# Four weight chunks of an expert kernel loaded in ten transfers each

## The reference

```
logits = xt @ w_router + b_router
top_val, top_idx = lax.top_k(logits, 4)            # 4 of 32 experts for each token
gates = softmax(top_val)
# for each expert e and its tokens xb:
h = xb @ w_gate_up[e] + b_gate_up[e]               # 1024 -> 2048
gate, up = minimum(h[:, :1024], 7), clip(h[:, 1024:], -7, 7)
out = ((up + 1) * gate * sigmoid(1.702 * gate)) @ w_down[e] + b_down[e]
y[token] += gates * out
```

## Time and profile before

| | us |
|---|---|
| median of 3 runs | 1215.03 (1214.45 to 1215.11) |
| the profiled execution | 1215.55 |
| its span, first to last instruction | 1213.8 |
| PE busy in the span | 1157.7 |
| PE waiting for DMA, 550 to 1190 us | 34.9 |

### The profile page before, as it was taken

One profiled execution on the slowest core, in us unless ns is written; L12 is line 12 of the kernel. 1 busy time (PEld: TensorE's weight loads), 2 busy tenths in 40 slices (PEclk: granted clock), 3 DMA queues, 4 the chain that ended last, 5 costly groups with the idle time before them and its releaser, 6 DMA issues.

```text
span 1213.8 us, 14228 instructions
## 1 busy us (share of the span) xinstructions
PE 1157.7 (95%) x5861; PEld 613.1 (51%) x5861; DVE 301.0 (25%) x700; ACT 143.0 (12%) x284; POOL 45.2 (4%) x80
## 2 busy tenths in 40 slices
PE   9999999999999999999998998989998989899996
PEld 7888678886434445353434343434343434354332
DVE  4343311223122222222222122211221212122212
ACT  2122111002010100001010101010101010001112
POOL 3032410000000000000000000000000000000000
PEclk9999999999999999999999999999999999999999
DMA  9753775484999999999999999999999999999995
GB/s 319 244 208 95 243 258 221 139 345 174 414 427 426 421 426 431 426 431 430 429 430 425 431 427 435 425 435 422 434 425 433 427 432 427 435 424 430 426 420 224
DMA packets 59884, 451.31 MB, mean 372 GB/s; under 512 B 3778, under 2 KB 34798, under 8 KB 40353
## 3 DMA queue, kind: packets, MB, share of 16 engines
q1 hardware_dynamic: 56576, 439.60, 87.4%
q0 software_dynamic: 2896, 10.11, 2.4%
q10 hardware_dynamic: 344, 0.61, 0.1%
HBM read 444.46 MB, written 6.08 MB: 371 GB/s over the span
## 4 chain that ended last, share of the span: by engine, by line
PE 73%; DMA 22%; SPq 2%; issue 1%; DVE 1%; ACT 0%; POOL 0%; DVEq 0%; POOLq 0%
PE psum L1040 30%; DMA ring<-in_w_gate_up 20%; PE psum L976 19%; PE psum L1051 7%; PE psum L1115 7%; PE psum L1143 2%; SPq L561 2%; DMA ring<-in_w_down 2%; PE psum L1105 1%; PE psum L1144 1%; PE psum L1041 1%; PE psum L842 0%; PE psum L857 0%; PE psum L1141 0%; PE psum L830 0%
## 5 line engine op out<-in xcount | busy, mean ns | idle before, releaser
L1040 PE MATMUL psum<-ring,x_T 128*64 128x512 f32 x992 | 458.4, 611 | 26.3 <-DMA ring<-in_w_gate_up 19.4
L1041 PE MATMUL psum<-ring,x_T 128*64 128x512 f32 x992 | 458.6, 611 | 0.0
L1040 PEld LDWEIGHTS psum<-ring,x_T 128*64 128x64 f32 x992 | 131.6, 140 | 285.2 <-issue 273.1
L1051 PE MATMUL psum<-ring,act_T 128*64 128x512 f32 x960 | 212.6, 595 | 14.5 <-DMA ring<-in_w_down 14.5
L976 PE MATMUL psum<-ring 128*128 128x264 f32 (+1 forms) x768 | 182.0, 392 | 0.6 <-issue 0.6
L976 PEld LDWEIGHTS psum<-ring 128*128 128x128 f32 x768 | 143.3, 190 | 30.3 <-issue 4.2
L1051 PEld LDWEIGHTS psum<-ring,act_T 128*64 128x64 f32 x960 | 68.9, 137 | 144.9 <-issue 133.0
L1041 PEld LDWEIGHTS psum<-ring,x_T 128*64 128x64 f32 x992 | 131.8, 140 | 0.0
L1828 DVE TENSOR_TENSOR hidden<-psum,params 128x512 f32<-128x512 f32 x32 | 22.1, 691 | 309.2 <-PE psum L1105 309.2
L1115 PE MATMUL psum<-one_hot,normed 128*128 128x128 f32 x768 | 91.5, 276 | 0.6 <-DVE one_hot L1728 0.6
L1115 PEld LDWEIGHTS psum<-one_hot,normed 128*128 128x128 f32 x768 | 88.5, 192 | 5.0 <-issue 5.0
(11 more groups left out here) (263 smaller groups left out, 658.9 us busy)
## 6 DMA issues: line engine op xcount, KB each, us to landing
ring<-in_w_gate_up SPq DMA_DIRECT2D x44, 4096.0 KB, 30.6
ring<-in_w_down SPq DMA_DIRECT2D x56, 2048.0 KB, 33.0
ring<-in_w_gate_up SPq DMA_DIRECT2D x40, 2048.0 KB, 16.2
ring<-in_w_in SPq DMA_DIRECT2D x21, 1024.0 KB, 5.7
ring<-in_w_down SPq DMA_DIRECT2D x12, 1024.0 KB, 29.2
out<-ring POOLq DMA_DIRECT2D x9, 512.0 KB, 5.1
ring<-in_state_ret POOLq DMA_DIRECT2D x8, 512.0 KB, 7.2
ring<-in_w_ret_branch SPq DMA_DIRECT2D x4, 1024.0 KB, 5.1
```

The costliest lines, as they stand in the source:

```text
L1040: mm(psum[0:CAP, 2 * j + n], x, gate, start=first, stop=final)
L1041: last = mm(psum[CAP:P, 2 * j + n], x, up, start=first, stop=final)
L1051: last = mm(psum[j * CAP:(j + 1) * CAP, 4 + n], hidden[:, j, 4 * h + i], w, start=h == 0 and i == 0, stop=h == 1 and i == 3)
```

## The change

In pairs 1 and 2, where each w_gate_up chunk is a load of its own, four of them, (1,9), (1,11), (2,1) and (2,9), are no longer loaded by one transfer of 128 rows. Each now takes ten: seven transfers of 16 rows, the i-th with rows i, i+8, i+16 and so on for i = 0 to 6, and three that share out the remaining rows 7, 15, 23 to 127, in transfers of 6, 6 and 4 rows. Each of the four chunks has a semaphore of its own, lumped_in, to which every one of the ten transfers adds 16, and PE waits for 160. The other chunks, all slots and PE's program are as before.

```diff
+LUMPED = ((1, 9), (1, 11), (2, 1), (2, 9))
+LUMPS = ((0, 6), (6, 12), (12, 16))
+IN_LUMPED = 7 + len(LUMPS)
...
 def signal(p, c):
 
+    if (p, c) in LUMPED:
+        return "lumped", LUMPED.index((p, c))
     return ("pair", chunk_slot(p, c - BODY[c][2] % 2)) if as_pair(p, c) else ("one", chunk_slot(p, c))
...
+        lumped_in = [sem(f"lumped_in{s}") for s in range(len(LUMPED))]
...
             key = (kind, s)
+            if kind == "lumped":
+                pe.wait_ge(lumped_in[s], 16 * IN_LUMPED * (r + 1))
+                return
             pe.wait_ge((pair_in if kind == "pair" else expert_in)[s],
...
                 sp.dma_start(slot(s, 2), src).then_inc(pair_in[s], 16)
+                return
+            if (p0, c) in LUMPED:
+                landed = lumped_in[LUMPED.index((p0, c))]
+                rows, to = gate_up_rows(2 * p + j, k), slot(s)
+                for i in range(7):
+                    sp.dma_start(to[i:P:8], rows[i:P:8]).then_inc(landed, 16)
+                for a, b in LUMPS:
+                    sp.dma_start(to[8 * a + 7:8 * b:8], rows[8 * a + 7:8 * b:8]).then_inc(landed, 16)
                 return
```

## The result

The changed kernel takes 1250.76 us (median of 4 runs, 1249.59 to 1253.32), the kernel before 1215.05 us beside it: a ratio of 1.0298, 95% interval 1.0285 to 1.0310, or +35.7 us. The prediction was 1227.8 us, slower, with a range from 1212 to 1238. The direction and the place are right; the size is not, and the time lies outside the range.

The account below looks back on a forecast made before the run. The prediction took the DMA stream of expert weights from 332 us on as the bound. Slow pieces at +15.2 us and moved rows at -2.4 summed to +12.8, giving 1227.8 us, with a range from 1212 to 1238.

Parts of the forecast that it names:

- step (4): Rows moved between engines by the 6, 6 and 4 row transfers: -2.4 us, with +4.9 as the other end.
- step (5): 28 pieces of 16 rows at state_pool's 227 GB/s, engines sharing a way into SBUF two to one: +15.2 us.
- What bounds the kernel: From 332 us the expert weights are one unbroken DMA stream at 428 GB/s, share 1.00; its last byte sets the end.
- Step (1): Same bytes, slots and place of PE's wait, now on each chunk's own semaphore: cost 0.
- Step (2): 36 more DMA issues on SP at 0.45 us each, covered by the queue: 0, up to 3 us.
- Step (3): Small transfers as such: at most 0.02 us more per 256 KB piece, 0.7 us for 40, taken as 0.
- engines in step: Within step (5): all engines do step i at about the same time, which speaks for the 15.2 us.
- bound from b_down: Price of the 28 pieces from the slowed stream around b_down's load: 0.42 us lost for 128 KB, 24 us in all.
- A: Rival: engines share no way in, only step (4)'s balance is left, 1212.6 us; chance 0.24.
- B: Rival: no slow pieces, but engines landing last get more rows, end moves by 4.9 us to 1219.9; chance 0.07.
- C: Rival: engines drift a row or two apart within a chunk, pieces cost a third, 1217.7 us; chance 0.08.
- D: Rival: b_down's price and more for the pieces, and SP held besides, beyond 1240 us; chance 0.04.

Follow-up runs that it names:

- e10: The changed kernel with each of the four chunks in two transfers instead, even rows then odd rows: 1215.78 us, +0.8 us over the kernel before.
- e15: The changed kernel with each of the four chunks in four transfers of 32 rows, every fourth row, instead: 1216.10 us, +1.1 us over the kernel before.
- e2: The changed kernel with each of the four chunks in eight transfers of all 128 rows by an eighth of the columns: 1217.70 us, +2.5 over the kernel before.
- e1: The changed kernel with each of the four chunks in eight transfers of 16 rows (each eighth), none of 6 or 4: 1240.89 us, +25.7 over the kernel before.
- e8: The changed kernel with the last 16 rows of each chunk in two transfers of 8 instead of 6, 6 and 4: 1249.56 us, +34.6 over the kernel before.
- e14: The changed kernel with each chunk in six transfers of 16 rows and four of 8 rows (each fourth): 1253.18 us, +38.2 over the kernel before.
- e3: The changed kernel with only chunk (1,9) divided as in the change: 1222.68 us, +7.5 over the kernel before.
- e7: The changed kernel with only chunks (1,9) and (1,11) divided as in the change: 1230.36 us, +15.4 over the kernel before.
- e13: The changed kernel with only chunks (1,9), (1,11) and (2,1) divided as in the change: 1240.07 us, +25.1 over the kernel before.
- e9: The changed kernel with each of the four chunks in two transfers instead, rows 0-63 then 64-127: 1242.00 us, +27.0 over the kernel before.
- e5: The changed kernel with each chunk in eight transfers of 16 rows (each eighth), in order 0,4,1,5,2,6,3,7: 1233.68 us, +18.7 over the kernel before.
- e6: The changed kernel with only chunk (1,9) divided, in eight transfers of 16 rows (each eighth): 1221.36 us, +6.4 over the kernel before.
- e4: The changed kernel with only chunk (1,9) divided, in eight transfers of 16 consecutive rows: 1226.69 us, +11.5 over the kernel before.
- e12: The changed kernel with only chunk (1,9) divided, in sixteen transfers of 8 consecutive rows: 1243.55 us, +28.5 over the kernel before.

## Why the prediction was right and where it was wrong

The path and the direction were right. Two terms of the sum failed: step (4), which took the transfers of 6, 6 and 4 rows as costing nothing beside the next chunk and as a gain of 2.4 us, where they cost some 13 us; and step (5), which took 15.2 us for the pieces of 16 rows, where they cost some 22.5.

**What bounds the kernel**: right. The loss in the stream, 33.4 us, is the loss in the span, 34.0, and the share stayed at 1.00. PE's waits grew and begin before 550 us. They didn't grow "by about the loss" but by two thirds of it, since PE's own matmuls became 12 us longer at the lower clock, which the prediction leaves out. The stage from 332 to 400 us fell to 280 GB/s, not to about 350, at the share of 1.00 that was forecast.

**Step (1)**, bytes and waits 0: nothing speaks against it; e10 and e15 have the same own semaphores and cost about 1 us.

**Step (2)**, issues 0 up to 3: right in its outcome, wrong in its number. SP in the changed kernel (start, us, what):

```profile
333.32 4.41 SPq L560 DMA_DIRECT2D ring<-in_w_gate_up  x7
337.77 2.23 SPq L562 DMA_DIRECT2D ring<-in_w_gate_up  x3
340.05 0.43 SPq L565 DMA_DIRECT2D ring<-in_w_gate_up  x1
...
386.16 4.99 SPq L560 DMA_DIRECT2D ring<-in_w_gate_up  x7
391.20 3.30 SPq L562 DMA_DIRECT2D ring<-in_w_gate_up  x3
394.64 4.11 SPq L565 DMA_DIRECT2D ring<-in_w_gate_up  x2
398.80 4.24 SPq L669 DMA_DIRECT2D out_sq<-in_b_down  x1
```

Seven pieces take 4.41 us, 0.63 each, not 0.45, and the load behind the ten starts 6.7 us after the first. Later SP is held, up to 4.24 us for one issue, as the earlier trace rows had warned. The cover held all the same: no stage of the table from 332 to 450 us has a share under 0.99.

**Step (3)**, small transfers as such 0.02 us: too small. e2 puts 28 of them at 0.09 us each, and e15's twelve come to the same, with an interval that includes 0. At that price the 36 of the change are 3.2 us, an estimate, where I took 0 and 0.7 as the bound. The row of the tail, 416 against 428 GB/s, was read over 8 us with only a few small pieces in it.

**Step (4)**, moving rows, -2.4 us, with 0 for the pieces of 6, 6 and 4: wrong, and the step that cost most. I counted rows per engine and little else. By e1 the 28 sixteens cost 28/32 of 25.7 = 22.5 us, an estimate, which leaves 35.7 - 22.5 = 13.2 us for the last sixteen rows of the four chunks. My term was -2.4 (the bounds together +7.9). e8 shows that it isn't the number of rows for each engine, e14 that such transfers are dear even when their rows are spread, and e3, e7, e13 and the change that the later chunks cost more, some 4 us in all. I had charged these rows to "the other engines, beside the next chunk" at 0; that it is just the next chunk that is slowed fits the longer stretches, but isn't shown. Why such transfers are so dear stays open.

That some engines are behind the others, which the step supposed, can be seen at the end of the stream. The last load that PE waits for lands at 1197.8 us before and, by the chain of the changed kernel, at 1231.8. The rows are two of the kernel before, then that of the chain and one by stage of the changed kernel:

```profile
1185.80:1197.80 12.00, 11.94 (x56) 4.12 (x52) 0.00 (x0) 0.00 (x0) 0.00 (x0) 1.00 0.85 338
1194.00:1198.00 4.00, 3.94 (x20) 1.21 (x18) 0.00 (x0) 0.00 (x0) 0.00 (x0) 1.00 0.57 223
...
1212.09 19.75 DMA ring<-in_w_down
...
1219.80:1231.80 12.00, 11.96 (x54) 4.11 (x50) 0.00 (x0) 0.00 (x0) 0.00 (x0) 1.00 0.85 334
```

For its last 4 us the stream before keeps only 0.57 of the engines' time busy, so a good part of them has finished early, as the step supposed. But over the last 12 us the mean share is 0.85 in both kernels: moving the rows bought nothing there, and the gain of 2.4 us isn't seen.

**Step (5)**, 28 pieces at 0.54 us = 15.2: the rate was forecast well and the size wasn't. state_pool's 227 GB/s became 215 to 221 in three stretches, and my 220 to 240 for a chunk's pieces was nearly met. That is in part luck, since the row doesn't show state_pool alone. By queue, from 16.2 to 17.4 us of the kernel before (packets, MB, share; SP's queue first, then POOL's):

```profile
q1 hardware_dynamic: 150, 0.15, 56.3%
q0 software_dynamic: 47, 0.13, 45.4%
```

More than half of the engines' time went to another load, of SP, in packets of about 1 KB. Nor is it a case of the rule with which the prediction compares it: by the rule of ports in the Trainium skill, "SBUF — State Buffer", section "Door 1: The DMA port swizzle", rows 0 to 119 reach all 16 ports. The prediction's own reason, engines in step, failed where it was tested with larger transfers (e10).

What failed is the size: 22.5 us, 0.80 us a piece. The bytes of a piece at 215 instead of 428 GB/s are 0.61 us more, and I had reckoned with bytes alone. The small transfer adds 0.09. The rest, some 0.1 us a piece, goes with bytes that aren't the pieces': e9's first slow stretch moved 11 x 218 = 2.40 MB and the change's 2.63, the chunk being 2.1. That the *whole stream* is slow until the last engine is through with its pieces, and that engines arrive one after another, is my reading of this; no row shows it. The bound from b_down, 24 us, held for this step. A sentence in my text, "the whole stream slows down, not the one load", had it; the sum didn't.

**Engines in step**: half right at most. Theory 2 of e10 is refuted, and with e15 the picture in which engines meet because they take the same step at the same time, for transfers of 32 and 64 rows. For pieces of 16 rows the order does matter (e5, 7 us).

**Rivals.** A (balance alone, 1212.6) and B (wrong engines, 1219.9) fall with the rates: 215 GB/s is no matter of rows per engine. C (slip, 1217.7) was to leave a third of the price; the most that another order took off is 7 of 25.7 us (e5). D (beyond 1240) is the number that happened, given 0.04, but not its mechanism: with b_down's price for the pieces and the last rows the sum ends at 1239.6, SP held isn't seen to cost anything, and what lies beyond comes from the last sixteen rows. 12.8 - 35.7 = -22.9 us is missing in the sum: 7.3 in steps (5) and (3), 15.6 in step (4).

**Not settled**: why a transfer of 4 to 8 rows is so dear (e8, e14), which engines fall behind, why e9's halves cost 27.0 us where half rate explains 4 x 4.9 = 19.6, and whether it is the rows in SBUF or the rows in memory that count. No row shows the engines singly.

## What to carry to other kernels

Where DMA is the bound, cut a load by columns, or by every second or fourth row, not into neighbouring rows, each eighth row, or a few rows: here a chunk of 2 MB cost 0.2 to 0.6 us more in the first ways and 6 to 28 us more in the others. Price a transfer that doesn't spread over all partitions by what it does to everything else that is under way, not by its own bytes. And don't balance engines with small transfers before a run shows that they are free.

## What the runs showed of the hardware

- The rate of the whole stream follows the rows of the transfers under way: 428 GB/s for 128 rows, 420 to 430 for every second or fourth (e10, e15); 215 to 238 for each eighth row (e3, e6), 218 for 64 neighbours (e9); 135 for 16 neighbours (e4); 113 to 152 for 8 neighbours (e12).
- A row of 16 KB takes an engine 0.61 us, and 1.25 us in the mean while such pieces are under way (e3); the DMA share stays at about 1.00 either way.
- Order matters for sixteens: 0, 4, 1, 5 (e5) instead of 0, 1, 2, 3 (e6) gave 281 instead of 238 GB/s from 336 to 348 us.
- Transfers of 8 rows cost more than their bytes: two of them in place of one of 16 rows in each of four chunks cost 8.9 us (e8 against e1).
- A small transfer of all 128 rows in a full queue costs 0.09 us besides its bytes (e2), while SP needs 0.63 us to issue one with 16 spread rows (the change).
- PE gained 12.0 us of busy time at the same number of matmuls when its waits became longer (granted clock 0.74 to 0.90 in the stages from 390 to 450 us).
